# Regrouping the cached-page attention of a one-layer hybrid step, and the order of its first jobs

## What is computed

```python
def gather_pages(cache_l, page_table):
    pages = cache_l[page_table]
    return pages.reshape(pages.shape[0], pages.shape[1] * pages.shape[2], *pages.shape[3:])
# trunk_layer
h = rmsnorm(x, norm_mix)                 # x * rsqrt(mean(x*x) + EPS) * g
z = h @ w_in
ka_all = jnp.concatenate([pa_k.astype(ka.dtype), ka], axis=1)
...
# dsa_attention (a), for the selected keys ks and values vs of a query
logits = jnp.einsum('bqgrd,bqngd->bqgrn', qg, ks).reshape(b, qb, H_A, n_sel) * (DH ** -0.5)
logits = jnp.where(valid[:, :, None, :], logits + bias, -jnp.inf)
p = jax.nn.softmax(logits, axis=-1).reshape(b, qb, HKV_A, grp, n_sel)
o = jnp.einsum('bqgrn,bqngd->bqgrd', p, vs)
# the sum of the three
m = (jax.nn.sigmoid(g_a) * (o_a @ w_pa) + jax.nn.sigmoid(g_b) * (o_b @ w_pb)
     + jax.nn.sigmoid(g_c) * (o_c @ w_pc))
```

## Time and profile before

| | us |
|---|---|
| median of 3 runs | 2428.72 (2427.34 to 2429.49) |
| the profiled execution | 2429.12 |
| its span, first to last instruction | 2427.4 |
| PE busy | 2391.0 (99%) |
| DVE busy | 1410.1 (58%) |
| ACT busy | 918.2 (38%) |
| POOL busy | 313.1 (13%) |
| HBM read and written | 425.27 MB and 27.52 MB, 187 GB/s |

### The profile page before, as it was taken

How to read it: one execution, slowest core, us unless ns; L and a number is a source line. 1 busy time by engine, 2 the same in 40 slices (tenths; PEclk the granted TensorE clock), 3 DMA queues, 4 the chain that set the end, 5 groups by cost and what they waited for, 6 DMA issues and landing times.

```text
span 2427.4 us, 44519 instructions
## 1 busy us (share of the span) xinstructions
PE 2391.0 (99%) x17208; PEld 2293.7 (94%) x17208; DVE 1410.1 (58%) x2093; ACT 918.2 (38%) x1274; POOL 313.1 (13%) x626
## 2 busy tenths in 40 slices
PE   8999999999999999999999999999999999999997
PEld 7978999999999888888899999999999999999997
DVE  5545568899887544344445655656654346666443
ACT  5334343333433444334333344333333333333332
POOL 1135110000002222333200011000000000000001
PEclk9999999999999999999999999999999999999999
DMA  6447545556558888989676544444445544444553
GB/s 230 143 130 238 176 138 179 179 167 208 197 174 273 298 275 280 304 283 318 229 259 192 187 155 148 148 153 151 147 143 152 151 149 154 148 148 154 145 151 104
DMA packets 174386, 458.69 MB, mean 189 GB/s; under 512 B 24970, under 2 KB 74490, under 8 KB 174048
## 3 DMA queue, kind: packets, MB, share of 16 engines
q1 hardware_dynamic: 141040, 372.31, 47.1%
q0 software_dynamic: 26080, 75.67, 9.6%
q10 hardware_dynamic: 7056, 7.88, 0.9%
HBM read 425.27 MB, written 27.52 MB: 187 GB/s over the span
## 4 chain that ended last, share of the span: by engine, by line
PE 92%; DMA 2%; issue 2%; DVE 1%; ACT 1%; POOLq 1%; POOL 0%; DVEq 0%; SPq 0%; ACTq 0%
PE ps L778 85%; PE ps L1004 1%; DMA vpg<-in_cache_b_v 1%; PE ps L1045 1%; PE ps L851 1%; ACT w_hi L1086 1%; DMA vpg<-in_cache_a_v 1%; POOLq L675 0%; PE ps L1027 0%; PE ps L975 0%; DMA xT<-in_x 0%; PE ps L967 0%; PE ps L863 0%; POOL vpg L676 0%; PE ps L918 0%
## 5 line engine op out<-in xcount | busy, mean ns | idle before, releaser
L1333 DVE TENSOR_TENSOR w_lo<-w_raw,w_hi 128x1024 fp32r<-128x1024 f32 (+1 forms) x622 | 750.5, 1207 | 813.4 <-ACT w_hi L1086 808.5
L778 PE MATMUL ps<-h_hi,w_hi 128*128 128x320 f32 x3696 | 1161.2, 314 | 12.6 <-DVE w_lo L1333 11.5
L778 PE MATMUL ps<-h_hi,w_lo 128*128 128x320 f32 x3696 | 1142.8, 309 | 0.0
L778 PE MATMUL ps<-h_lo,w_hi 128*128 128x320 f32 x3696 | 1142.6, 309 | 0.0
L1086 ACT ACTIVATE w_hi<-w_raw 128x1024 fp32r<-128x1024 f32 (+1 forms) x622 | 647.5, 1042 | 817.7 <-PE ps L778 799.3
L778 PEld LDWEIGHTS ps<-h_hi,w_hi 128*128 128x128 f32 x3696 | 694.8, 188 | 51.6 <-issue 48.0
L778 PEld LDWEIGHTS ps<-h_lo,w_hi 128*128 128x128 f32 x3696 | 694.9, 188 | 0.7
L778 PEld LDWEIGHTS ps<-h_hi,w_lo 128*128 128x128 f32 x3696 | 694.4, 188 | 0.0
L778 PE MATMUL ps<-y_hi,w_hi 128*128 128x320 f32 x688 | 212.8, 309 | 1.5 <-DVE yt L1405 1.5
L778 PE MATMUL ps<-y_hi,w_lo 128*128 128x320 f32 x688 | 212.6, 309 | 0.0
L778 PE MATMUL ps<-y_lo,w_hi 128*128 128x320 f32 x688 | 212.6, 309 | 0.0
(11 more groups left out here) (320 smaller groups left out, 2019.6 us busy)
## 6 DMA issues: line engine op xcount, KB each, us to landing
w_raw<-in_w_in SPq DMA_DIRECT2D x258, 512.0 KB, 4.8
w_raw<-in_ffn_up SPq DMA_DIRECT2D x86, 512.0 KB, 3.8
w_raw<-in_ffn_gate SPq DMA_DIRECT2D x86, 512.0 KB, 3.6
w_raw<-in_ffn_down SPq DMA_DIRECT2D x80, 448.0 KB, 3.4
kpg<-in_cache_b_k SPq DMA_DIRECT2D x128, 128.0 KB, 4.2
vpg<-in_cache_b_v POOLq DMA_DIRECT2D x128, 128.0 KB, 4.8
kpg<-in_cache_a_k SPq DMA_DIRECT2D x128, 128.0 KB, 4.1
vpg<-in_cache_a_v POOLq DMA_DIRECT2D x128, 128.0 KB, 4.6
```

Of the source, the lines that this page charges most:

```text
L778: mm = mmul(bank[q][:, 0:T], wp[:, s, cols], xp[:, x.k0 + k, :], start=(x.first and k == 0 and t == 0), stop=(x.last and k == x.nk - 1 and ...
L1333: tt(w_lo[:, s, 0:n], w_raw[:, s, 0:n], w_hi[:, s, 0:n].bitcast(F32), ALU.subtract).then_inc(w_lo_done, 1)
```

## The change

- **Start.** The first four jobs (`ki`, `qi0`, `qi1`, `qi2`) are done by turns: their four first halves, then their four second halves. SP loads weights 1 to 3 ahead of the third and fourth part of x; ACT and DVE prepare units 2 and 3 after block 7. POOL's first loads wait for the third part of x instead of the second. DVE adds the squares to one block (two more additions, of 640 and 320 columns), with no `low` in between, and PE's sum is one matmul instead of four.
- **Keys.** All four lots and the own keys stand ahead of unit 0. In a the four masks follow them, and only then is a lot reported as used (`lg_ps`). DVE takes all maxima ahead of its first `dense`. ACT computes the exponentials after `dense(2)`, between `high(4)` and `high(5)`.
- **Values.** PE transposes two quarters ahead of unit 5; two more and the own part, and then the first two products, ahead of unit 6; the other two ahead of unit 10. ACT's and DVE's copies stand at units 5 and 6.
- **Page numbers.** POOL reads the four page numbers of a lot before it waits for the lot's slot.

```diff
@@ Job / all_units
+        self.turns = 4 if kind == "ki" else 2 if self.opens else 1
@@ SP, start
             features(1)
-            transfer(1)
+            for v in range(1, 4):
+                transfer(v)
             features(2)
             features(3)
-            for v in range(2, SP_LEAD):
+            for v in range(4, SP_LEAD):
                 transfer(v)
@@ POOL
-            pool.wait_ge(x_arrived[1], 16)
+            pool.wait_ge(x_arrived[2], 16)
...
+                    pages = []
+                    for s in range(2):
+                        for j in range(2):
+                            k = (2 * p + s) * NPG + 2 * c + j
+                            pages.append(pool.value_load(pt_sb[0:1, k:k + 1], min_val=0, max_val=NPOOL - 1))
                     if lot >= V_LOTS:
                         pool.wait_ge(v_used, lot - V_LOTS + 1)
@@ PE, start
-            for k in range(4):
-                mm = mmul(bank[2][:, 0:T], ones[:, :], sqx[:, k, :], start=(k == 0), stop=(k == 3))
-            mm.then_inc(n_sum, 1)
+            mmul(bank[2][:, 0:T], ones[:, :], sqx[:, 0, :], start=True, stop=True).then_inc(n_sum, 1)
@@ PE, sample
-                    if mx == 0:
-                        mm = mmul(bank[2 + c], ecur[:, p, :], m16[:, c * 512:(c + 1) * 512], start=False, stop=True,
-                                  skip_group_check=True)
-                    if c < 3:
+                    if mx == 1 and c < 3:
                         mm.then_inc(lg_ps, 1)
-                        dense(1)
...
-                dense(3)
+                dense(5)
                 pe.wait_ge(ex_done, x + 1)
-                for c in range(5):
...
+                for two in range(3):
+                    for c in (2 * two, 2 * two + 1):
...
-                    dense(1)
+                    dense((1, 4, 1)[two])
@@ ACT, start
                 if k == 7:
                     high(1)
-            high(2)
+                    high(2)
+                    dense(1)
+            dense(1)
@@ ACT, sample
-                dense(4)
+                dense(2)
                 act.wait_ge(mx_done, x + 1)
...
-                dense(2)
+                dense(3)
@@ DVE, start
+                V(tt(sqx[:, 0:4, :], sqx[:, 0:4, :], sqx[:, 4 * g:4 * g + 4, :], ALU.add))
+            V(tt(sqx[:, 0:2, :], sqx[:, 0:2, :], sqx[:, 2:4, :], ALU.add))
+            tt(sqx[:, 0, :], sqx[:, 0, :], sqx[:, 1, :], ALU.add).then_inc(x_sqs, 1)
+            dense(2)
```

More of the change, by code:

```diff
@@ L108, in all_units @@
         units.append([Unit(job, at, a, b - a) for a, b in zip(ends[:-1], ends[1:])])
[L109 to L114, removed]
+    out, at = [], 0
+    while at < len(jobs):
+        turns = jobs[at].turns
+        out += [x for some in zip(*units[at:at + turns]) for x in some]
+        at += turns
     return out
@@ L673, in _ @@
                         for j in range(2):
-                            k = (2 * p + s) * NPG + 2 * c + j
-                            page = pool.value_load(pt_sb[0:1, k:k + 1], min_val=0, max_val=NPOOL - 1)
+                            page = pages[2 * s + j]
                             pool.dma_start(vpg[:, lot % V_LOTS, s, j, :], a[("cache_a_v", "cache_b_v")[mx]][0]
@@ L996, in sample @@
                     pe.wait_ge(k_in[lot % K_LOTS], 128 * (lot // K_LOTS + 1))
-                    if x:
+                    if x and c == 0:
                         pe.wait_ge(pT_even, 2 * x)
@@ L1018, in sample @@
                 if mx == 0:
-                    mm = mmul(bank[6][:, 0:P], ecur[:, p, :], m16[:, PAST:L].unsqueeze(1).to_broadcast([P, 2 * NB, TS]),
+                    for c in range(4):
+                        mm = mmul(bank[2 + c], ecur[:, p, :], m16[:, c * 512:(c + 1) * 512], start=False, stop=True,
+                                  skip_group_check=True)
+                        if c < 3:
+                            mm.then_inc(lg_ps, 1)
+                    mm = mmul(bank[6][:, 0:P], ecur[:, p, :],
+                              m16[:, PAST:L].unsqueeze(1).to_broadcast([P, 2 * NB, TS]),
                               start=False, stop=True, skip_group_check=True)
                 mm.then_inc(lg_ps, 1)
-                dense(3)
+                dense(5)
                 pe.wait_ge(ex_done, x + 1)
-                for c in range(5):
[L1025 to L1030, removed]
+                for two in range(3):
+                    for c in (2 * two, 2 * two + 1):
+                        if c < 4:
+                            for j in range(4):
+                                mm = turn(bank[2 + c][:, j * P:(j + 1) * P], pr[:, (4 * c + j) * P:(4 * c + j + 1) * P],
+                                          ident[:, :])
+                            mm.then_inc(t_ps, 1)
+                    if two == 1:
                         turn(bank[6][:, P:2 * P], pn[:, :], ident[:, :]).then_inc(t_ps, 1)
-                    if c >= 1:
-                        j = c - 1
+                    for j in (2 * two - 2, 2 * two - 1) if two else ():
                         if j % 2:
@@ L1049, in sample @@
                                 mm.then_inc(v_used, 1)
-                    if c == 4:
+                    if two == 2:
                         pe.wait_ge(pT_odd, 3 * x + 3)
@@ L1292, in sample @@
                         .then_inc(ex_done, 1)
-                dense(2)
[L1294 to L1298, removed]
+                dense(3)
+                for c in (0, 2):
+                    act.wait_ge(t_ps, 5 * x + c + 1)
+                    act.wait_ge(v_used, 8 * x + c)
+                    fn(flat(pT[:, 0, :, :]), bank[2 + c], ACT.Copy).then_inc(pT_even, 1)
                     dense(1)
+                dense(4)
                 act.wait_ge(ot_ps, x + 1)
@@ L1704, in sample @@
                 V(nc.vector.reciprocal(total[:, 10:11], total[:, 9:10]))
[L1705 to L1709, removed]
+                for c in (1, 3):
+                    dve.wait_ge(t_ps, 5 * x + c + 1)
+                    dve.wait_ge(v_used, 8 * x + (4 if c == 3 else 0))
+                    copy(flat(pT[:, 1, :, :]), bank[2 + c]).then_inc(pT_odd, 1)
                     if c == 3:
```

18 lines of the change are left out of this document (8 added, 10 removed).

## The result

| | us |
|---|---|
| before, median of 7 runs | 2428.72 (2427.01 to 2429.49) |
| changed, median of 7 runs | 2437.42 (2435.07 to 2439.66) |
| ratio | 1.0037, 95% interval 1.0025 to 1.0049 |
| changed, the profiled execution | 2438.96 |
| its span | 2437.2 |

The change makes the kernel slower by 0.37%, where the prediction had 1.8 us less, with 2437 as the upper end of its range. Most of what it expected came in; one wait, for which it had put in 0.8 us, was 10.4.

What follows compares the result with a forecast made beforehand. PE, busy 99% of the span, was taken as the bound. Terms of 22.2 us less and 20.4 more gave 1.8 less: 2427.3 profiled, 2426.9 median; own range 2422 to 2432, 8-in-10 range 2416 to 2437.

Steps and rivals of the forecast that it cites:

- start: Start of the kernel: a wait, seven-block sum of squares matmuls and idle at the reciprocal shrink or go, 3.6 us less.
- merged keys and values: All eight rounds: fewer changes between small matmuls and units, 1.75 or 1.65 us per round, 13.6 us less (11 to 15).
- value pages: PE's waits for value lots 6 and 7 at the fourth product go, 5 us less.
- keys of round 0: Round 0: PE stands for the fourth key lot, wanted at 776.2 but landing at 784.5, 8.3 us more.
- half clock in rounds 0 and 1: Behind round 0's stand: 14 matmuls at half clock, 1.7 us more (0 to 2).
- bank ahead of unit 4: Rounds 1 to 3: unit 4 waits 2.5 us each for a late evacuation, 7.5 us more, plus 0.5 in round 0.
- unit 8 of round 6: Round 6: PE's wait for the first new block shows in full, 2.3 us instead of 0.65, 1.6 us more.
- keys of rounds 6 and 7, half clock behind them: Rounds 6 and 7: late keys from more loads on SP's queue and busy DMA, 0.8 us more (0 to 3).
- Keys late in every round: Rival: pages land 2 us later still in seven rounds, up to 14 us, 2441; half the rounds, 2434; chance 0.18.
- The bank is free in time: Rival: ACT and DVE run some 2.5 us earlier, so unit 4's 7.5 us go, 2419; chance 0.22.
- No half clock: Rival: the clock does not fall after round 0's stand, 1.7 us less, 2425.2; chance 0.12.
- No value wait regained: Rival: round 0's stand alone, later value slots again filled too late, 5 us more, 2431.9; chance 0.06.

Runs made afterwards that it cites:

- experiment 1: The changed kernel with the 2.56 MB load of `oc_f` issued in eight parts of 320 KB, one ahead of each lot of value pages in round 5: 2430.06 us.
- experiment 2: The changed kernel with the load of `oc_f`, in one piece, issued ahead of round 5's value pages instead of round 6's: 2439.72 us.
- experiment 4: The changed kernel with ACT's exponentials one unit later in the b rounds, between `high(5)` and `high(6)`: 2431.83 us.
- experiment 7: The changed kernel with `oc_f` in eight parts, b's exponentials one unit later, and round 0's fourth key lot two units behind the third: 2414.29 us, ratio 0.9946.
- experiment 3: The changed kernel with POOL reading each value page's number right before its load again, as in the kernel before: 2436.66 us.
- experiment 6: The changed kernel with SP issuing the last 16 key pages of round 0 one unit earlier: 2436.87 us.
- four edits: The changed kernel with `oc_f` in eight parts, b's exponentials later, round 0's fourth key lot later, SP's key pages over units 1 to 10: 2409.91 us, ratio 0.9930.

## Why the prediction was wrong

| term | predicted | measured in the trace |
|---|---|---|
| start | -3.6 | -4.0 |
| merged keys and values | -13.6 | -13.3 |
| value pages | -5 | -4.1 |
| keys of round 0 | +8.3 | +6.6 |
| half clock in rounds 0 and 1 | +1.7 | +4.7 |
| bank ahead of unit 4 (0.5 of it in round 0) | +8.0 | +6.6 |
| unit 8 of round 6 | +1.6 | +0.6 |
| keys of rounds 6 and 7, half clock behind them | +0.8 | +10.4, +0.3, +2.1 |
| sum | -1.8 | +9.9 |

The profiled executions differ by 2438.96 - 2429.12 = 9.8 us, so the terms close the account; that of the merged pieces is taken from a b round and an a round and multiplied. The wait of 0.5 us that the prediction added in round 0 did not come. Two of its small sums are off without changing anything: 3 x 0.31 is 0.93 and not 0.95, and 24 matmuls of 0.148 us are 3.54, while the 3.52 that it uses for a unit is what its timeline rows give.

**The step that failed** is the one sentence "for late keys there I add 0.8 (0 to 3)". It was worth 12.8 us, and those 12 us are nearly the whole error of 11.7; the other terms' errors cancel. Three things went into it. The place was named ("a busy DMA", with more loads on SP's queue) but its row was not read: landing times of key pages were taken from round 0, 4.7 to 5.4 us, and used for all rounds, while the trace of before had loads of up to 12.6 us at exactly this place, beside the load of `oc_f`. Next, the deadline moved up by 11.5 us in every round, and a landing that is late by 7 us is hidden before and bare after. And last, even those rows of before were too kind, for the change itself makes SP later in the a rounds. There the last page was issued at 1096.9, 9.2 us ahead of the round (1106.1), and the lot was complete at 1109.55; its new hour would have been 1106.1 + 3 x 0.88 = 1108.8, so by them it is 0.8 us late. In the changed kernel the last page was issued at 1100.97, 4.6 us ahead of the round (1105.59), and took 17.7 us. In between stands SP, which had waited for the masks of round 5 and then issues three pages every 3.8 to 4.3 us without a pause. Experiments 1 and 2 show that it takes the large load: with SP as late as that, and landings of 4.2 us, the round has no wait. How much of the 10.4 us belongs to SP's lateness beside the load was not tried; by the rows of before, with SP earlier beside the same load (issued 3.3 us later), it would have been the 0.8 us.

**Rivals.** "Keys late in every round" had the right mechanism, SP's last pages against a deadline 11.5 us earlier, and the right side, with the wrong shape: not some 2 us in seven rounds but 10.4 in one and 0.3 in another. In rounds 3 and 7 of the changed kernel the lot lands within 0.3 us of its hour, and experiments 4 and 7 made that margin visible as waits of 0.2 to 1.0 us. "The bank is free in time" fell: all three waits are there, 2.2 us each instead of 2.5, and experiment 4 removes them by moving their cause. "No half clock" fell too. "No value wait regained" fell.

**What was right.** Start, merges, value waits, round 0's stand and the bank chain are each within 1.7 us, and their waits stand, or are gone, where the prediction said. Round 0's stand was 1.7 shorter since SP issued at 771.36 in a round that began at 769.54, 1.8 us into it where it had been 2.5 (775.99 and 773.53), and the pages took 4.2 us instead of 5.2. Unit 8 of round 6 waits 1.24 where the prediction had 2.3 in full, and its row stands against the earlier trace rows:

```profile
1156.41 0.38 PE L784 MATMUL ps<-h_hi,w_hi 128*128 128x320 f32 x1 [1.24 <-DVE h_lo L1672]
```

**The clock's share was mis-sized**, 1.7 against 4.7 us, and 6.8 with round 6's. The prediction took the slow stretch from the start of the kernel, 14 matmuls, and one stand. But in rounds 0 and 6 the lower level came within the stand (in round 1 behind it), and what is left of it behind the stand is what costs: 6 us behind 6.6 us of stand in round 0, 4 us behind 10.4 in round 6. The trace gives no rule by which a longer stand costs more.

**The clock and the DMA queues.** The Trainium skill has two statements that bear on them. On its page "TensorE: Matmul & The Clock Gate", section "Part 1: The HAM clock gate", it says that the gate watches activity in periods that run on by themselves and don't start with the kernel's work, so that the number of slow matmuls changes between runs of one kernel. No run shows such periods, but what the profiles show agrees with it: the same stand of 2.2 us ahead of unit 4 in round 1 brought the lower level in the profiles of the changed kernel and of experiments 1 and 2 (0.96 over 830 to 870 us), and not in those of experiments 3 and 6 (1.00), and in none of the five behind the like stands of rounds 2 and 3. On the page "DMA: Bandwidth & Descriptors" of the Trainium skill, section "Queues, rings and completion order", it says that each DMA engine goes round between the queues that have work for it, a packet at a time. By that a large load is no wall for the small ones, but takes a share of their rate for as long as it lasts. The rows agree. Between 1082 and 1122 us POOL's queue (q0, with `oc_f` and the values) and SP's (q1, with keys and weights) had nearly the same share of the 16 engines:

```profile
q0 software_dynamic: 2063, 6.82, 46.6%
q1 hardware_dynamic: 3361, 5.81, 43.0%
```

Between 1086 and 1106 us SP's queue moved 2.79 MB, against 4.39 MB in experiment 1; from 1090 us on the engines were full in both (a DMA share of 1.01 to 1.04 up to 1105 us). So SP's rate fell by about a third. The landing times grew by more, page by page, as SP went on issuing: pages issued from 1084 to 1088 us took 4.0 to 5.6 us, from 1088 to 1092 up to 10.3, from 1092 to 1096 up to 14.0, and the last one 17.7, although `oc_f` itself had landed at 1106.0. That looks like a backlog in SP's own queue, which is longest for the page issued last, the very one that PE waits for; no run tries this apart from the large load.

## What to carry to other kernels

When an edit moves up the time at which data is wanted, the price is not the mean landing time but the longest one in each stretch, read beside whatever large transfer runs there; list the landings round by round and set them against the new hour. Look also at what the edit does to the release of the slots, for it can make the loads later at the same time. A large load with a late deadline is best cut into parts and put behind the small urgent ones: here that alone was worth 7.4 us of 2437 by medians and 10.4 by profiles. And a regrouping that costs more than it brings may have its gain in many small places and its loss in few: here four edits turned 0.37% slower into 0.70% faster.

## What the runs showed of the hardware that was not expected

- A stand of PE of 2.2 us can bring the lower clock for a little over 3 us (some 1.7 us lost), in three of the five profiles that have the same stand in round 1, and not behind the like stands of rounds 2 and 3. Medians of kernels with such stands are the less certain for it.
- One load of 2.56 MB on another queue stretched the landing of 128 KB loads from 4.2 to between 14.2 and 17.7 us, and the longest came for the page issued last, 12 us after the large load's issue. The same bytes in eight parts, one with each lot of value pages, left them at 4.1 to 4.6 us in the round that mattered, and cost 1.7 us where the parts ran.
- Pages issued 3.1 us earlier landed 1.6 us earlier: part of an earlier issue was lost in a longer landing (5.8 us instead of 4.2 for the last page).
